# Two-way gated memory of a mixer stage: one triangle over 512 tokens, or two halves with a state across them

## The chip, the cores and the metric

One program runs on one core of one Trainium2 chip. The metric is the device time of a run in microseconds (us). Besides the times there is one profiled run, read here as "the trace". Its times count from the first instruction.

## The reference, cut to what matters

The kernel computes two transformer blocks on 512 tokens of width 1024. The change is in one mixer of the second block, a matrix memory (mLSTM) that runs over the tokens forwards and, a second time, backwards. Eight heads, keys and queries of 64, values of 128:

```python
def step(carry, inp):
    C, n, m = carry
    ...
    s = jnp.einsum('bhtd,bhsd->bhts', qj, kj) * jnp.exp(D - m_t[..., None])
    num = jnp.einsum('bhts,bhsv->bhtv', s, vj) + w_inter[..., None] * jnp.einsum('bhvd,bhtd->bhtv', C, qj)
    den = jnp.sum(s, axis=-1) + w_inter * jnp.einsum('bhd,bhtd->bht', n, qj)
    h = num / jnp.maximum(jnp.abs(den), jnp.exp(-m_t))[..., None]
    ...
    C = decay[..., None, None] * C + jnp.einsum('bhsv,bhsd->bhvd', vj * wk[..., None], kj)
...
h_fwd = mlstm_chunkwise(q, k, v, g[0, 0], jax.nn.log_sigmoid(g[0, 1]))
h_bwd = flip(mlstm_chunkwise(flip(q), flip(k), flip(v), flip(g[1, 0]), flip(jax.nn.log_sigmoid(g[1, 1]))))
hs = (h_fwd + h_bwd).transpose(0, 2, 1, 3).astype(h.dtype)
hs = rms_norm(hs) * head_gain
```

The result does not depend on the chunk: a chunk of 512 needs no state at all, a chunk of 256 needs one state per head and direction.

## The kernel before

Five engines run five queues written out by hand; semaphores order them. **Weights** come in units of 1024 x 256. For unit m, SP loads `raw` (`load(m)`), ScalarE writes its rounded high part (`high(m)`, L839), GpSimd the low part in two halves (`low(m)`, L660), and TensorE multiplies with three matmuls for each tile (L2440 to L2442). Each of raw, high and low has two buffers: `high(m)` waits until TensorE is done with unit m-2. `load(m)` waits for `low(m-2)`. A unit starts on TensorE when its high part and the first half of its low part are there (`unit_ready`).

**The stage od_in** has units n to n+12. n to n+4 give queries, keys (256 features each pair of units) and gates; n+5 to n+8 the output gate `mo`; n+9 to n+12 the values `vx`, each unit for two heads. Gate rows are made by VectorE during n+6 (`gate_rows`): `irow` (log weight of a token as a source), `Mrow` (running maximum), `erow`. After unit n+8 TensorE transposes `irow` (L3234) and then `erow` (L3238), which count `r_tr` to 1 and 2. ScalarE's queue around this is `high(n+8)`, the exponential of `erow` (L1391), two sigmoids of `mo` (L1375), `high(n+9)`, another sigmoid, four silus of `cy` (queries and keys, L1371), `high(n+10)`. SP copies `Mrow` to DRAM (`mrows`) after `load(n+11)` and then reads its 16 rows back, each broadcast to 128 partitions (L642, ring of four).

**The heads.** For head h and direction d (0 forwards, 1 backwards):

- ScalarE (L1431) writes four blocks of weights `wt`, exp(row + column), for the source block j of 128 tokens against all targets at its side: 512, 384, 256, 128 wide forwards, and the reverse backwards. Four sets `wt[s % 4]` exist, s = 2h + d; set s waits for `l_o`, the outputs of s-4.
- GpSimd zeroes half of each diagonal block (L801, 8 a head). Its queue in head h: the 8 selects, `mo` times the gain (L804), in heads 0, 3 and 5 `low(n+11)`, `low(n+12)`, `low(n+13)`, and from head 2 `gated_head(h-2)` (L793).
- TensorE makes scores (L3287), four matmuls 64 rows deep and 512 wide, one in each of banks 0 to 3; `scores_half(h+1, 0)` and `(h+1, 1)` stand in head h. VectorE multiplies weights by scores (`decayed`, L2340, 8 a head), counted by `l_a`.
- TensorE sums (`out_rows(h, d)`, L3273): ten matmuls 128 x 129 over the ten blocks of the triangle. They wait for `l_a` and for `l_h`, VectorE's `heads_out` of the direction before (L2349 to L2359), which empties banks 6 and 7.
- Between these TensorE works off units n+10 to n+12, a third of a block at a time (`next(beside)`): chunks a, b, c of 15, 15 and 18 matmul triples for heads 0 to 5. At the start of a unit it waits for its whole low part (`unit_whole`). Heads 6 and 7 have no such filling.
- VectorE in head h: `decayed` 0 to 4, a copy of values (`take_values`, L2302, heads 1 to 6), `decayed` 5, `heads_out(h-1, 1)`, `decayed` 6 and 7, `heads_out(h, 0)`, and the norm of older heads (`head_sums`, `normed_head`). In head 7 `heads_out(6, 1)` stands after `decayed` 3.
- ScalarE in head h: weights of h, in heads 0, 3, 5 `high(n+11)`, `high(n+12)`, `high(n+13)`, then squares and roots of older heads.

After head 7 come transposes of the normed heads (L3299) and the stage od_out, whose first unit is L2491 and L2496.

Of the kernel before, what the change touches and what calls it, by code (L numbers as in the profile page):

```python
# [220 lines left out]
def bass_block_pair(nc, a, out):  # L221
# [163 lines left out]
    hgain = place("hgain", [P, D], F32, AR + 49408)[0]  # L385
    wt = []
    for i in range(4):
        offset = [ULOFF + 5120 * i] * TB
        for j in range(1, TB):
            offset[j] = offset[j - 1] + 512 * (TB - j + 1 if i % 2 == 0 else j)  # L390
        if i == 3:
            offset = [AR + 57088, ULOFF + 15360, AR + 55552, AR + 53504]
        wt.append([place(f"wt{i}{j}", [P, (TB - j if i % 2 == 0 else j + 1) * P], F32, offset[j])[0] for j in range(TB)])
    cy = place("cy", [P, KC, S], F32, UHOFF)[0]
# [6 lines left out]
    erow = place("erow", [64, S], F32, SQOFF[1])[0]  # L401
    bcr = R + sq
    mrows = nc.dram_tensor("mrows", [64, S], F32, kind="Internal").ap()
    ccol = place("ccol", [P, TB, 64], F32, SSOFF)[0]
    ecol = place("ecol", [P, TB, 64], F32, GSOFF)[0]

# [10 lines left out]
    with ExitStack() as ctx:  # L417
# [13 lines left out]
        def sem(name):  # L431
# [73 lines left out]
        def _(sp):  # L505
# [148 lines left out]
        def _(pool):  # L654
# [164 lines left out]
        def _(act):  # L819
# [580 lines left out]
            nc.scalar.activation(ccol[:], ps[6][:, 0:256].rearrange("p (a b) -> p a b", a=TB), ACT.Copy).then_inc(r_cols, 1)  # L1400
            nc.scalar.activation(ecol[:], ps[7][:, 0:256].rearrange("p (a b) -> p a b", a=TB), ACT.Copy).then_inc(r_cols, 1)
            act.wait_ge(r_cols, 2)

# [17 lines left out]
            nc.scalar.preload_act_table_set("natural_log_exp_and_others")  # L1421
            for h in range(ML_H):
                for d in range(2):
                    s = 2 * h + d
                    act.wait_ge(bc_in[s % BC_RING], 16 * (s // BC_RING + 1))
                    if s >= 4:
                        act.wait_ge(l_o, s - 3)
                    for j in range(TB):
                        lo, hi = (j * P, S) if d == 0 else (0, (j + 1) * P)
                        row = h + 32 * d  # L1430
                        nc.scalar.activation(wt[s % 4][j][:], bcr[s % BC_RING][:, lo:hi], ACT.Exp,  # L1431
                                             bias=ccol[:, j, row:row + 1]).then_inc(l_w, 1)
                if h in (0, 3, 5):
# [23 lines left out]
        def _(dve):  # L1457
# [847 lines left out]
            def gate_rows():  # L2305
# [73 lines left out]
            def mixed_low(j):  # L2379
                low_op(Q0["od_mix"] + j, uL[:, j, :], ps[MIX_BANK[j]][:], uH[:, j, :])  # L2380

            for h in range(ML_H):
                tail = h == ML_H - 1
                for x in range(2 * TB):
                    decayed(8 * h + x)
                    if x == 4 and 1 <= h <= 6:
# [39 lines left out]
        def _(pe):  # L2426
# [795 lines left out]
            for u in range(5, 10):  # L3222
# [8 lines left out]
                if u == 8:  # L3231
# [5 lines left out]
                    for tb in range(TB):  # L3237
                        ins = nc.tensor.transpose(ps[7][:, tb * 64:(tb + 1) * 64], erow[:, tb * P:(tb + 1) * P], ident[0:64, 0:64])  # L3238
                    ins.then_inc(r_tr, 1)
            pe.wait_ge(blk_taken, TAKEN[V_FILL[0]])  # L3240
            pe.wait_ge(r_cols, 2)

# [18 lines left out]
            def out_rows(h, d):  # L3261

                pe.wait_ge(l_a, 8 * h + 4 * d + 4)
                if 2 * h + d:
                    pe.wait_ge(l_h, 2 * h + d)
                if h % 2 == 0 and h and d == 0:
                    pe.wait_ge(blk_taken, TAKEN[V_FILL[0] + h])
                for i in range(TB):
                    dst = ps[6 + i // 2][:, (i % 2) * 129:(i % 2) * 129 + 129]
                    js = range(0, i + 1) if d == 0 else range(i, TB)  # L3270
                    for j in js:
                        at = (i - j if d == 0 else i) * P
                        ins = nc.tensor.matmul(dst, wt[(2 * h + d) % 4][j][:, at:at + P], vx[:, j, h, :],  # L3273
                                               start=(j == js[0]), stop=(j == js[-1]))
                ins.then_inc(l_o, 1)

            pe.wait_ge(c_silu, KC)

            def scores_half(h, d):

                if h >= ML_H:
                    return
                hp = (h % 2) * 64
                for j in range(2 * d, 2 * d + 2):
                    if h:
                        pe.wait_ge(l_a, 8 * (h - 1) + 4 + j + 1)
                    nc.tensor.matmul(ps[j][:], cy[hp:hp + 64, 4 + h // 2, j * P:(j + 1) * P], cy[hp:hp + 64, h // 2, :],  # L3287
                                     start=True, stop=True).then_inc(l_qk, 1)

            def head_transposes(j):  # L3290
# [10 lines left out]

            scores_half(0, 0)
            scores_half(0, 1)
            beside = values_beside()
            for h in range(ML_H):
                next(beside, None)
                scores_half(h + 1, 0)
                next(beside, None)
                if h == ML_H - 1:
                    head_transposes(0)  # L3310
                    head_transposes(1)
                out_rows(h, 0)
                scores_half(h + 1, 1)
                next(beside, None)
# [91 lines left out]
```

## Time and profile before

| | us |
|---|---|
| median of 3 runs | 2059.47 |
| lowest, highest | 2057.3, 2065.16 |
| the profiled execution, first to last instruction | 2057.0 |
| its stretch from the first scores to the first matmul of od_out | 1524.38 to 1645.13 |

The profile gives no separate time of its own run; its span lies 2.5 us below the median. Views used: the page (shares, slices), the chain that ended last in order of time, timelines of one engine (a line that says x20 merges 20 records and its time runs from the first start to the last end), tables of short windows with the granted TensorE clock, and groups of instructions. A matmul in plain fp32 leaves two records, so ten matmuls of `out_rows` are x20.

### The profile page before, as it was taken

The numbers are of one execution on the slowest core, as the hardware profiler recorded it, in microseconds if no ns is written. First come the engines' busy times: TensorE is split into PE (matmuls) and PEld (weight loads), VectorE is DVE, ScalarE is ACT, GpSimd is POOL, SyncE is SP. The second block draws the span as 40 slices with busy tenths as digits, with TensorE's granted clock in tenths as the row PEclk, the third lists the DMA queues.
The fourth block names the chain that finished last, engine by engine and source line by source line (L and its number), as shares of the span: only waits on it lengthen the run. The fifth ranks groups of instructions, "written<-read, shape, count | busy, mean of one in ns | idle before, by whom it ended". The sixth has DMA issues, their size and how long they took to land.

```text
span 2057.0 us, 25915 instructions
## 1 busy us (share of the span) xinstructions
PE 2010.6 (98%) x10087; PEld 1672.1 (81%) x10087; DVE 1199.0 (58%) x1955; ACT 752.2 (37%) x1029; POOL 906.8 (44%) x500
## 2 busy tenths in 40 slices
PE   8999899999999999999999999999999899999998
PEld 6877788988888888877788788888888788888887
DVE  6454657646789895688578877516656752111112
ACT  5344534333513222447542122125353344222121
POOL 3422424754445444346244444445454345444442
PEclk9999999999999999999999999999999999999999
DMA  4322203516577862240348778423341023322321
GB/s 152 102 84 82 77 2 102 165 62 155 146 195 180 200 168 83 82 138 21 87 120 203 187 182 199 128 73 113 103 127 61 21 83 103 103 89 96 103 92 72
DMA packets 227823, 233.41 MB, mean 113 GB/s; under 512 B 6891, under 2 KB 222772, under 8 KB 227580
## 3 DMA queue, kind: packets, MB, share of 16 engines
q1 hardware_dynamic: 227216, 231.72, 40.1%
q8 instruction: 77, 1.26, 0.3%
q14 instruction: 38, 0.31, 0.1%
q10 hardware_dynamic: 492, 0.12, 0.0%
HBM read 229.56 MB, written 2.24 MB: 113 GB/s over the span
## 4 chain that ended last, share of the span: by engine, by line
PE 88%; DVE 7%; issue 2%; ACT 1%; DMA 1%; POOL 1%; SPq 0%; DVEq 0%; ACTq 0%
PE ps L2440 22%; PE ps L2442 21%; PE ps L2441 21%; PE ps L2491 7%; PE ps L2496 3%; DVE adacc L1985 2%; PE ps L3287 1%; PE ps L3273 1%; PE ps L2946 1%; PE ps L2877 1%; POOL wL L660 1%; PE ps L2728 1%; PE ps L2907 1%; DVE ssum L1478 1%; DMA raw<-in_w_in_dram 0%
## 5 line engine op out<-in xcount | busy, mean ns | idle before, releaser
L660 POOL TENSOR_TENSOR wL<-raw,wH 128x1024 fp32r<-128x1024 f32 (+2 forms) x320 | 769.3, 2425 | 948.7 <-ACT wH L839 883.6
L839 ACT ACTIVATE wH<-raw 128x2048 fp32r<-128x2048 f32 (+2 forms) x160 | 300.8, 1880 | 433.3 <-PE ps L2442 331.4
L2440 PE MATMUL ps<-uH,wH 128*128 128x512 f32 x1088 | 425.5, 391 | 3.0 <-DVE uL L1528 0.9
L2442 PE MATMUL ps<-uH,wL 128*128 128x512 f32 x1088 | 423.5, 389 | 0.0
L2441 PE MATMUL ps<-uL,wH 128*128 128x512 f32 x1088 | 423.4, 389 | 0.0
L1985 DVE SCALAR_TENSOR_TENSOR adacc<-adaw,adab,adacc 128x256 f32<-128x256 f32 x372 | 307.6, 827 | 12.9
L2440 PE MATMUL ps<-hnH,wH 128*128 128x512 f32 x728 | 287.7, 395 | 2.2 <-DVE xT L1597 1.7
L2442 PE MATMUL ps<-hnH,wL 128*128 128x512 f32 x728 | 283.8, 390 | 0.0
L2441 PE MATMUL ps<-hnL,wH 128*128 128x512 f32 x728 | 283.2, 389 | 0.0
L2440 PEld LDWEIGHTS ps<-uH,wH 128*128 128x128 f32 x1088 | 204.2, 188 | 46.9 <-issue 3.4
L2442 PEld LDWEIGHTS ps<-uH,wL 128*128 128x128 f32 x1088 | 204.2, 188 | 43.0
L2441 PEld LDWEIGHTS ps<-uL,wH 128*128 128x128 f32 x1088 | 204.3, 188 | 41.9
L2211 DVE TENSOR_TENSOR T<-ps,R 128x512 f32<-128x512 f32 x44 | 30.2, 690 | 280.5 <-PE ps L2442 269.6
L2440 PEld LDWEIGHTS ps<-hnH,wH 128*128 128x128 f32 x728 | 137.0, 188 | 31.4 <-issue 4.1
L2442 PEld LDWEIGHTS ps<-hnH,wL 128*128 128x128 f32 x728 | 136.6, 188 | 28.9
L2441 PEld LDWEIGHTS ps<-hnL,wH 128*128 128x128 f32 x728 | 136.8, 188 | 28.5 <-issue 1.0
L1597 DVE SCALAR_TENSOR_TENSOR xT<-ps,mod,xT 128x512 f32<-128x512 f32 x64 | 47.0, 748 | 148.2 <-PE ps L2442 108.6
L2440 PE MATMUL ps<-wH,hnH 128*128 128x256 f32 x384 | 111.9, 292 | 0.0
L2442 PE MATMUL ps<-wH,hnL 128*128 128x256 f32 x384 | 109.2, 284 | 0.0
L2441 PE MATMUL ps<-wL,hnH 128*128 128x256 f32 x384 | 109.2, 284 | 0.0
L2491 PE MATMUL ps<-hnH,wH 128*128 128x512 f32 x264 | 105.0, 398 | 2.9 <-ACT hnH L888 2.9
L2491 PE MATMUL ps<-hnH,wL 128*128 128x512 f32 x264 | 103.9, 393 | 0.0
(478 smaller groups left out, 3035.3 us busy)
## 6 DMA issues: line engine op xcount, KB each, us to landing
raw<-in_ffn_w_dram SPq DMA_DIRECT2D x60, 1024.0 KB, 5.4
adaw<-in_ada_w_dram SPq DMA_DIRECT2D x192, 256.0 KB, 7.1
raw<-in_w_dram SPq DMA_DIRECT2D x32, 1024.0 KB, 5.5
raw<-in_w_in_dram SPq DMA_DIRECT2D x14, 1024.0 KB, 5.3
raw<-in_od_w_in_dram SPq DMA_DIRECT2D x12, 1024.0 KB, 5.3
raw<-in_w_xkv_dram SPq DMA_DIRECT2D x16, 512.0 KB, 3.6
raw<-in_ffn_w_dram SPq DMA_DIRECT2D x8, 768.0 KB, 4.2
raw<-in_ev_w_in_dram SPq DMA_DIRECT2D x5, 1024.0 KB, 5.3
```

The lines of the kernel that those rows point to most:

```text
L660: nc.gpsimd.tensor_tensor(wL[n % 2][:, k0:k1, 0:c], raw[n % 2][:, k0:k1, 0:c], wH[n % 2][:, k0:k1, 0:c].bitcast(F32), ALU.subtract).then_i ...
L839: nc.scalar.activation(wH[n % 2][:, 0:kc, 0:c], raw[n % 2][:, 0:kc, 0:c], ACT.Copy).then_inc(w_hi, 1)
L1478: nc.vector.tensor_tensor(acc[:], acc[:], sq[q % 2][:], ALU.add).then_inc(sq_added, 1)
L1597: nc.vector.scalar_tensor_tensor(out=xT[:, j, :], in0=ps[b % 4][:], scalar=gate(j), in1=xT[:, j, :], op0=ALU.mult, op1=ALU.add).then_inc(b ...
L1985: ins = nc.vector.scalar_tensor_tensor(out=acc, in0=adaw[m % ADA_RING][:, k, :], scalar=by, in1=acc, op0=ALU.mult, op1=ALU.add)
L2211: nc.vector.tensor_tensor(T[(q0 + c) % 2][:], ps[b % 4][:], R[c][:], ALU.mult).then_inc(blk_taken, 1)
L2440: nc.tensor.matmul(out_ap, wh, xh, start=first, stop=False)
L2441: nc.tensor.matmul(out_ap, wh, xl, start=False, stop=False)
L2442: return nc.tensor.matmul(out_ap, wl, xh, start=False, stop=last)
L2491: nc.tensor.matmul(ps[(BLOCK0[n] + c) % 4][:, 0:tokens], w[n % 2][:, k, cs], xh[:, k, :], start=w is wH and k == 0, stop=False)
L2496: ins = nc.tensor.matmul(ps[(BLOCK0[n] + c) % 4][:, 0:tokens], wH[n % 2][:, k, cs], xl[:, k, :], start=False, stop=k == kc - 1)
L2728: ins = nc.tensor.transpose(ps[6 + g % 2][:, j * P:(j + 1) * P], pr[g % PR_RING][:, j * P:(j + 1) * P], ident)
```

## The change

The tokens are cut into two halves of 256. Inside a half, weights and scores are as before, but only 256 and 128 wide. Across the halves a state of 64 x 129 for each head and direction carries the other half's sum.

```diff
 def scores(h, half):
-    nc.tensor.matmul(ps[j][:], cy[hp:hp + 64, 4 + h // 2, j * P:(j + 1) * P], cy[hp:hp + 64, h // 2, :], ...)
+    nc.tensor.matmul(ps[(2 * h + half) % 3][:, (j % 2) * 2 * P:(j % 2 + 1) * 2 * P],
+                     cy[hp:hp + 64, 4 + h // 2, j * P:(j + 1) * P], cy[hp:hp + 64, h // 2, t0:t0 + 2 * P], ...)
 def out_rows(h, d):
+    for i in (0, 1, 2, 3) if d == 0 else (2, 3, 0, 1):
+        js = range(i // 2 * 2, i + 1) if d == 0 else range(i, i // 2 * 2 + 2)
+        across = i // 2 != d
...
+        if across:
+            if i % 2 == 0:
+                pe.wait_ge(l_kq, ML_H // 2 + h // 2 + 1)
+                pe.wait_ge(h_st, 3 * HG_H + h + 1)
+            ins = nc.tensor.matmul(dst, decayed_queries(h // 2)[hp:hp + 64, i, :], cst_[hp:hp + 64, h // 2 % 2, d, :], ...)
+def states(h):
+    if h % 2 == 0 and h:
+        pe.wait_ge(blk_taken, TAKEN[V_FILL[0] + h])
+    for d in range(2):
+        for j in (2 * d, 2 * d + 1):
+            ins = nc.tensor.matmul(ps[3][hp:hp + 64, ...], weighted_keys(h // 2)[:, j, hp:hp + 64], vx[:, j, h, :], ...)
+    ins.then_inc(h_sp, 1)
```

TensorE's order in head h is now a, `scores(h+1, 0)`, b, `states(h)`, `out_rows(h, 0)`, `scores(h+1, 1)`, c, `out_rows(h, 1)`. Ahead of head 0 it transposes the keys (16 of 128 x 128), and, after unit n+9, `irow` again (4). VectorE weights the keys (4 of 128 x 512, from PSUM) and the queries (4 of 128 x 512); SP stores two decay rows (`erows`) and reads them back in eight broadcasts of 128 KB. ScalarE gets four exponentials on rows, two copies `wcol`, and `states_copy(h)`. Its queue:

```diff
             act.wait_ge(r_rows, 1)
             nc.scalar.activation(erow[:], erow[:], ACT.Exp, scale=-1.0).then_inc(r_em, 1)
+            act.wait_ge(r_rows, 2)
+            nc.scalar.activation(Erow[0:ML_H, 2 * P:S], Mrow[0:ML_H, 2 * P:S], ACT.Exp, bias=rcol[0:ML_H, 0:1]).then_inc(r_em, 1)
...
+            act.wait_ge(r_tr, 1)
+            nc.scalar.activation(irow[0:ML_H, 0:2 * P], irow[0:ML_H, 0:2 * P], ACT.Exp, ...).then_inc(r_em, 1)
...
             output_gate(0)
             output_gate(1)
             high(n+9)
...
+            gate_weights(0)
+            for h in range(ML_H):
+                states_copy(h)
+                if h + 1 < ML_H:
+                    gate_weights(h + 1)
                 if h in (0, 3, 5):
                     high(n + 11 + h // 2)
```

ScalarE, between units n+8 and n+9, before (`wH_51` is written by `high(n+8)`, `wH_52` by `high(n+9)`):

```order
673 L839 ACTIVATE wH_51<-raw_49 128x2048
674 L1391 ACT_TABLE_LOAD
675 L1391 ACTIVATE erow<-erow 64x512
676 L1375 ACT_TABLE_LOAD
677 L1375 ACTIVATE mo<-mo 128x4x256 x2
678 L839 ACTIVATE wH_52<-raw_50 128x2048
```

and now:

```order
673 L867 ACTIVATE wH_51<-raw_49 128x2048
674 L1419 ACT_TABLE_LOAD
675 L1419 ACTIVATE erow<-erow 64x512
676 L1421 ACTIVATE Erow<-Mrow,small 8x256
677 L1422 ACTIVATE Erow<-Mrow,small 8x256
678 L1425 ACTIVATE irow<-irow,Mrow 8x256
679 L1427 ACTIVATE irow<-irow,Mrow 8x256
680 L1403 ACT_TABLE_LOAD
681 L1403 ACTIVATE mo<-mo 128x4x256 x2
682 L867 ACTIVATE wH_52<-raw_50 128x2048
```

Four exponentials stand ahead of the sigmoids and of `high(n+9)`; the first on `irow` (row 678) carries the wait for `r_tr` 1.

ScalarE, end of the weights of head 0 and start of those of head 1, before (`wt_196` to `wt_199` are head 0's backward set, `wt_200` to `wt_203` head 1's forward set, `wH_52` is `high(n+11)`):

```order
694 L1431 ACTIVATE wt_198<-R_71,ccol 128x384
695 L1431 ACTIVATE wt_199<-R_71,ccol 128x512
696 L839 ACTIVATE wH_52<-raw_50 128x2048
697 L1431 ACTIVATE wt_200<-sq_72,ccol 128x512
698 L1431 ACTIVATE wt_201<-sq_72,ccol 128x384
```

and now:

```order
699 L1472 ACTIVATE wt_198<-R_71,ccol 128x128
700 L1472 ACTIVATE wt_199<-R_71,ccol 128x256
701 L1480 ACTIVATE cst__208<-ps 64x258
702 L1472 ACTIVATE wt_200<-sq_72,ccol 128x256
703 L1472 ACTIVATE wt_201<-sq_72,ccol 128x128
704 L1472 ACTIVATE wt_202<-sq_72,ccol 128x256
705 L1472 ACTIVATE wt_203<-sq_72,ccol 128x128
706 L1472 ACTIVATE wt_204<-sq_73,ccol 128x128
707 L1472 ACTIVATE wt_205<-sq_73,ccol 128x256
708 L1472 ACTIVATE wt_206<-sq_73,ccol 128x128
709 L1472 ACTIVATE wt_207<-sq_73,ccol 128x256
710 L867 ACTIVATE wH_52<-raw_50 128x2048
```

`high(n+11)` moved from ahead of head 1's weights to behind them, and all of these behind the copy of head 0's states (row 701). GpSimd's queue has the same order as before. In it `low(n+11)`, which needs `high(n+11)`, stands ahead of head 1's selects:

```order
220 L829 AFFINE_SELECT wt_199<-wt_199 128x128
221 L832 TENSOR_TENSOR mo<-mo,hgain 128x4x128
222 L688 TENSOR_TENSOR wL_54<-raw_50,wH_52 128x1024 x2
223 L829 AFFINE_SELECT wt_200<-wt_200 128x128
224 L829 AFFINE_SELECT wt_201<-wt_201 128x128
```

## Rows read from the trace of the kernel before

**Rows 1.** The page: engine totals; shares of the chain that ended last.
```profile
PE 2010.6 (98%) x10087; PEld 1672.1 (81%) x10087; DVE 1199.0 (58%) x1955; ACT 752.2 (37%) x1029; POOL 906.8 (44%) x500
PE 88%; DVE 7%; issue 2%; ACT 1%; DMA 1%; POOL 1%; SPq 0%; DVEq 0%; ACTq 0%
```
**Rows 2.** The last chain, 1511 to 1648: start us, length us, what.
```profile
1511.20 0.39 PE ps L3234 x4
...
1511.84 0.31 PE ps L2440
...
1523.57 0.77 DVE vx L2302 x2
1524.38 4.67 PE ps L3287 x8
...
1537.08 2.23 PE ps L3273 x20
1539.32 1.91 PE ps L3287 x4
...
1609.18 2.23 PE ps L3273 x20
...
1640.39 0.87 DVE hs L2359 x3
...
1645.13 0.93 PE ps L2491 x4
...
1647.89 0.44 PE ps L3299 x4
```
**Rows 3.** Timeline of ScalarE: start us, length us, what [idle before <-releaser].
```profile
1492.14 1.28 ACT L1375 ACT_TABLE_LOAD   x1
1493.43 2.01 ACT L1375 ACTIVATE mo<-mo 128x1024 f32<-128x1024 f32 x2
1499.78 1.92 ACT L839 ACTIVATE wH<-raw 128x2048 fp32r<-128x2048 f32 x1 [4.33 <-PE ps L2442]
...
1600.35 1.91 ACT L1431 ACTIVATE wt<-R,ccol 128x512 f32<-128x512 f32 x4
```
**Rows 4.** Timeline of GpSimd.
```profile
1530.27 2.01 POOL L801 TENSOR_SCALAR_AFFINE_SELECT wt<-wt 128x128 f32<-128x128 f32 x8
...
1564.14 4.70 POOL L660 TENSOR_TENSOR wL<-raw,wH 128x1024 fp32r<-128x1024 f32 x2 [0.26 <-ACT wH L839]
1568.79 1.27 POOL L793 TENSOR_TENSOR hs<-hs,mo 128x512 f32<-128x512 f32 x1
```
**Rows 5.** Windows: stretch, us, busy of PE, PEld, DVE, ACT, POOL, PEclk, DMA.
```profile
21.00:22.00 1.00, 1.00 (x4) 0.83 (x3) 0.90 (x2) 0.58 (x1) 0.00 (x0) 0.65 0.79 209
...
1526.00:1527.00 1.00, 1.00 (x3) 0.37 (x2) 0.86 (x2) 1.00 (x4) 1.00 (x1) 0.98 0.95 182
...
1533.00:1534.00 1.00, 1.00 (x2) 0.33 (x1) 0.00 (x0) 0.00 (x0) 0.51 (x1) 0.60 1.00 339
...
1630.00:1640.00 10.00, 6.92 (x55) 6.46 (x56) 9.48 (x32) 3.19 (x6) 1.28 (x1) 1.00 0.01 2
```
**Rows 6.** Timeline of TensorE at the program's start.
```profile
17.05 0.77 PE L2491 MATMUL ps<-hnH,wH 128*128 128x512 f32 x1 [2.85 <-ACT hnH L888]
```
**Rows 7.** Timeline of VectorE around `heads_out(5, 1)`.
```profile
1615.60 1.88 DVE L2340 SCALAR_TENSOR_TENSOR wt<-ps,wt 128x512 f32<-128x512 f32 x5
...
1618.38 0.15 DVE L2349 SCALAR_TENSOR_TENSOR small<-ps,ecol 128x2 f32<-128x2 f32 x1
...
1620.53 1.16 DVE L2340 SCALAR_TENSOR_TENSOR wt<-ps,wt 128x384 f32<-128x384 f32 x2
```
**Rows 8.** Groups of instructions by shape, 1510 to 1645: busy us, mean ns.
```profile
L2340 DVE SCALAR_TENSOR_TENSOR wt<-ps,wt 128x512 f32<-128x512 f32 x16 | 10.9, 684 | 1.4 <-PE ps L3287 1.3
...
L2340 DVE SCALAR_TENSOR_TENSOR wt<-ps,wt 128x128 f32<-128x128 f32 x16 | 3.9, 284 | 1.3 <-PE ps L3287 1.3
```
**Rows 9.** DMA issues, 1495 to 1640: KB each, median us to landing.
```profile
R<-mrows SPq DMA_DIRECT2D x8, 256.0 KB, 3.4
```

More of the change, by code:

```diff
@@ L385, in bass_block_pair @@
     hgain = place("hgain", [P, D], F32, AR + 49408)[0]
[L386 to L393, printed above, removed]
+    wt = [[place(f"wt{i}{j}", [P, (2 - j % 2 if i % 2 == 0 else j % 2 + 1) * P], F32,
+                 ULOFF + 3072 * i + 1536 * (j // 2) + (1024 if i % 2 == 0 else 512) * (j % 2))[0] for j in range(TB)] for i in range(4)]
+    cst_ = place("cst_", [P, 2, 2, ML_V + 1], F32, ULOFF + 12288)[0]
     cy = place("cy", [P, KC, S], F32, UHOFF)[0]
@@ L1421, in _, with gate_weights @@
             nc.scalar.preload_act_table_set("natural_log_exp_and_others")
-            for h in range(ML_H):
+            def gate_weights(h):
                 for d in range(2):
@@ L2380, in mixed_low @@
                 low_op(Q0["od_mix"] + j, uL[:, j, :], ps[MIX_BANK[j]][:], uH[:, j, :])
+            dve.wait_ge(r_cols, 4)
+            dve.wait_ge(c_silu, KC)
+            for p in range(ML_H // 2):
+                keys_weighted(p)
+            queries_decayed(0)
             for h in range(ML_H):
@@ L3239, in _ @@
                     ins.then_inc(r_tr, 1)
+            pe.wait_ge(r_em, 5)
+            for tb in range(TB):
+                ins = nc.tensor.transpose(ps[4][:, tb * 64:(tb + 1) * 64], irow[:, tb * P:(tb + 1) * P], ident[0:64, 0:64])
+            ins.then_inc(r_tr, 1)
             pe.wait_ge(blk_taken, TAKEN[V_FILL[0]])
-            pe.wait_ge(r_cols, 2)
+            pe.wait_ge(r_cols, 4)
             def values_beside():
@@ L3275, in out_rows @@
-                ins.then_inc(l_o, 1)
+                for i in (0, 1, 2, 3) if d == 0 else (2, 3, 0, 1):
+                    dst = ps[6 + i // 2][:, (i % 2) * 129:(i % 2) * 129 + 129]
+                    js = range(i // 2 * 2, i + 1) if d == 0 else range(i, i // 2 * 2 + 2)
+                    across = i // 2 != d
+                    for j in js:
+                        at = (i - j if d == 0 else i % 2) * P
+                        ins = nc.tensor.matmul(dst, wt[(2 * h + d) % 4][j][:, at:at + P], vx[:, j, h, :],
+                                               start=(j == js[0]), stop=(j == js[-1] and not across))
+                    if across:
+                        if i % 2 == 0:
+                            pe.wait_ge(l_kq, ML_H // 2 + h // 2 + 1)
+                            pe.wait_ge(h_st, 3 * HG_H + h + 1)
+                        ins = nc.tensor.matmul(dst, decayed_queries(h // 2)[hp:hp + 64, i, :], cst_[hp:hp + 64, h // 2 % 2, d, :],
+                                               start=False, stop=True)
@@ new lines, in out_rows @@
+                ins.then_inc(l_o, 1)
+            def states(h):
+                hp = (h % 2) * 64
+                if h % 2 == 0 and h:
+                    pe.wait_ge(blk_taken, TAKEN[V_FILL[0] + h])
+                if h:
+                    pe.wait_ge(h_st, 3 * HG_H + h)
+                for d in range(2):
+                    for j in (2 * d, 2 * d + 1):
+                        ins = nc.tensor.matmul(ps[3][hp:hp + 64, d * (ML_V + 1):(d + 1) * (ML_V + 1)], weighted_keys(h // 2)[:, j, hp:hp + 64],
+                                               vx[:, j, h, :], start=(j == 2 * d), stop=(j == 2 * d + 1))
+                ins.then_inc(h_sp, 1)
@@ L3277, in _, with scores @@
             pe.wait_ge(c_silu, KC)
-            def scores_half(h, d):
+            def scores(h, half):
                 if h >= ML_H:
@@ L3283, in scores_half, with key_transposes @@
                 hp = (h % 2) * 64
[L3284 to L3287, printed above, removed]
+                if h == 1 and half == 0:
+                    pe.wait_ge(l_kq, 1)
+                if h and half:
+                    pe.wait_ge(l_a, 8 * (h - 1) + 6)
+                elif h >= 2:
+                    pe.wait_ge(l_a, 8 * (h - 1))
+                for j in range(2 * half, 2 * half + 2):
+                    t0 = half * 2 * P
+                    nc.tensor.matmul(ps[(2 * h + half) % 3][:, (j % 2) * 2 * P:(j % 2 + 1) * 2 * P],
+                                     cy[hp:hp + 64, 4 + h // 2, j * P:(j + 1) * P], cy[hp:hp + 64, h // 2, t0:t0 + 2 * P],
                                      start=True, stop=True).then_inc(l_qk, 1)
+            def key_transposes(p):
+                for tb in range(TB):
+                    ins = nc.tensor.transpose(ps[(2, 3, 6, 7)[p]][:, tb * P:(tb + 1) * P], cy[:, 4 + p, tb * P:(tb + 1) * P], ident)
+                ins.then_inc(r_tr, 1)
             def head_transposes(j):
@@ L3300, in head_transposes @@
                 ins.then_inc(n_tr, 1)
-            scores_half(0, 0)
-            scores_half(0, 1)
+            scores(0, 0)
+            scores(0, 1)
+            for p in range(ML_H // 2):
+                key_transposes(p)
             beside = values_beside()
@@ L3306, in _ @@
                 next(beside, None)
-                scores_half(h + 1, 0)
+                scores(h + 1, 0)
                 next(beside, None)
+                if h == 0:
+                    pe.wait_ge(l_kq, ML_H // 2)
+                states(h)
                 if h == ML_H - 1:
```

78 lines of the change are left out of this document (63 added, 15 removed).

## The prediction

> **What bounds the kernel now.** I read the page first: TensorE is busy for 98% of the span and carries 88% of the chain that ended last [rows 1]. So a matmul taken out is worth its time, and any hole put into TensorE's queue costs its length. Then the chain from 1511 to 1648 [rows 2], where all edited work lies. It has four parts. Unit n+9 runs from 1511.84 to 1523.5. The first scores start at 1524.38, after VectorE's copy of values. Heads 0 to 5 repeat every 14.42 us (first `out_rows` of head 0 at 1537.08, of head 5 at 1609.18), and TensorE never waits there. From then on heads 6 and 7 have no filling: VectorE is busy for 9.48 of 10 us and TensorE for 6.92 [rows 5], and the chain alternates between them until `heads_out(7, 1)` ends at 1641.26 and od_out runs from 1645.13 [rows 2].
>
> **TensorE's work in a head.** Two 512-wide scores take 1.91, ten matmuls of 129 columns 2.23, or 0.223 each [rows 2]. A period holds two of each, so the filling is 14.42 - 3.82 - 4.46 = 6.14 (a 1.9, b 1.9, c 2.3). Now each pair of scores is 256 wide: between 0.96 (by columns) and 1.91 (if a fixed part ruled); I take 1.0, since 129-wide matmuls at 0.223 show hardly a fixed part. `out_rows` has six matmuls inside and two across: 8 x 0.223 = 1.8. `states` adds 4 x 0.223 = 0.9. No row has a stationary operand 64 columns wide, but the scores are 64 rows deep; I bound one between 0.11 and 0.3. The period becomes 6.1 + 2.0 + 3.6 + 0.9 = 12.6, 1.8 less, or 9.1 for the five from head 0 to head 5.
>
> **The opening,** from the first scores to the end of `out_rows(0, 0)`: 14.9 before (to 1539.31 [rows 2]). Now scores 2.0, 16 key transposes at 0.11 (four take 0.44 [rows 2]) 1.8, a 1.9, scores 1.0, b 1.9, states 0.9, `out_rows` 1.8: 11.4. That is -3.5, nearly all because the granted clock stood at half from 1527 to 1533.6 before [rows 5] (3.3 lost); that loss may come again (rival 2). Beside it VectorE weights four keys and one pair of queries, each a pass over 512 columns like `decayed` at 0.68 [rows 8] (bounds 0.4 to 0.9), 3.4 in all, under 9 us of TensorE. The four transposes of `irow` (0.39 [rows 2]) and two small copies stand ahead of the first scores, but in parallel with the 0.77 copy of values: +0.1. SP's eight further broadcasts are half the size of those that land in 3.4 [rows 9] and are needed some 5 us after the first scores: nothing.
>
> **The hole ahead of unit n+9.** This is the step that I weigh most. ScalarE's exponential on `irow` waits for `r_tr` 1, since it overwrites what TensorE transposes. That transpose starts at 1511.20 and takes 0.39 [rows 2]. Queued behind the wait are two sigmoids and `high(n+9)`, which before ran at 1499.78 [rows 3], beside unit n+8. Now: wait until 1511.6; two short exponentials 0.8 (nearest: four weight blocks in 1.91 [rows 3], bounds 0.4 to 1.0); table load 1.28; sigmoids 2.01; `high(n+9)` 1.92: 1517.7. GpSimd's first half of `low(n+9)` takes 4.70 / 2 [rows 4]: TensorE may start at 1520.1 in place of 1511.84, **+8.3**. Nothing else is at hand for TensorE. (The table load's row ends at 1493.42 and the sigmoid starts at 1493.43 [rows 3], so a switch costs 1.28 here. The Trainium skill, "ScalarE: Activation LUTs", "What ACT_TABLE_LOAD costs", puts a drain of about 1.38 us on top of each switch; by that the hole would be 9.7 and the sum 1.4 higher. The row has no room for it, so I go by the row.) Later work catches up during the unit: four silus, `high(n+10)`, the last sigmoid and SP's broadcasts (held behind `load(n+11)`, which waits for `low(n+9)`, done at 1522.5) all end before the unit does at some 1534.
>
> **The clock behind it.** At the start of the program TensorE sat idle for 2.85 us, and its matmuls from 17.05 on ran at half the clock (1.2 of 2.4 GHz) until 21.65 [rows 5, 6]: 4.6 us at half, 2.3 lost. An idle stretch of 8.3 will do the same: **+2.3**.
>
> **The holes in heads 1, 4 and 6.** ScalarE now writes the weights of head h+1 only after the copy of head h's states, and in heads 0, 3 and 5 `high` comes behind them. GpSimd's queue is unchanged, so head h+1's selects stand behind the `low` that waits for that `high`. From the end of `states(h)`: copy 0.4, eight weight blocks 3.0 (two sets at 1.5, since 1280 columns in 1.91 [rows 3] shrink to 768; bounds 2.3 and 3.8), `high` 1.9, `low` 4.7, in heads 3 and 5 `gated_head` 1.3, first select 0.3 [rows 4]. Then VectorE: `decayed` 0 to 4, values, `decayed` 5 took 2.78 (1615.60 to 1618.38 [rows 7]) and shed 0.5 (512 columns fewer forwards at 400 ns for 384 [rows 8]), 2.3; I allow 2.5 because the selects feed them at 0.25 each. Then `heads_out(h, 1)` 2.15 [rows 7]. Sum: 15.0 for h = 0, 16.3 for h = 3 and 5. `out_rows(h+1, 0)` waits for this `heads_out`. TensorE has 12.6 of its own work up to there, in head 5 only 12.6 - 3.8 = 8.8. So it stands 2.4 us in head 1 and 3.7 in head 4 (3.0 of these at the start of unit n+12, whose low part is late by the same chain): **+6.1**. In the kernel before ScalarE was a head ahead and none of these waits was late.
>
> **From `out_rows(5, 0)` to `out_rows(6, 0)`** before: 1611.41 to 1620.53, 9.1 (it waited for `heads_out(5, 1)` [rows 2, 7]). Now 16.3 - 1.8 = 14.5: **+5.3**, with TensorE idle for most of 7 us. From there to the end of `heads_out(7, 1)` the chain is VectorE's: head 7's weights are 1024 columns narrower (-1.0), one `out_rows` on the chain is shorter (-0.4): -1.5. Behind it nothing changes.
>
> **The clock in the tail.** It stayed at 1.00 there with TensorE 69% busy [rows 5]. Now a hole of 5 to 6 us comes first, as long as or longer than the one of rows 6. At half the clock `out_rows(6, 0)` costs 1.8 more; if the clock stays low to the end of the stage, each of four `out_rows` does, less their slack beside VectorE: 4.2. I take **+2.0**.
>
> **Sum against the profiled execution** (span 2057.0): 8.3 + 2.3 + 0.1 - 3.5 - 9.1 + 6.1 + 5.3 - 1.5 + 2.0 = +10.0: 2067.0. The median lies 2.5 above the span: 2069.5, with the upward bounds weighing more, **2070 us**, 0.5% more than before. About 0.5%, 10.3 us, is what a measurement of this kernel can tell from no change, so the forecast lies on that edge. Chance 0.45 for 2066 to 2073.
>
> **Rival 1, the saving comes through (faster).** TensorE sheds 3.5 + 9.1 + 1.5 with 0.1 added: -14, 2045.5. It decides for itself if ScalarE gets over the wait on `r_tr` without TensorE noticing, that is if `high(n+9)` need not wait, and if `low` is done before the selects are missed. For it: 98% busy TensorE [rows 1]. Against: both waits are plain in the queues, and the hole would need to be under a tenth of what I find. Chance 0.05. If only the holes in the heads fail to show (weights and `high` early enough), 8.3 + 2.3 + 0.1 - 3.5 - 9.1 - 1.5 = -3.4: 2056. Chance 0.10.
>
> **Rival 2, the clock falls more often.** The first scores again follow a gap and are light work; the clock may fall as at 1527 [rows 5], +3.3, and stay low through the tail, +2.2 more: 2075.5. For it: the same sequence did so before; against: the scores are half as long and followed by full-height transposes. Chance 0.22.
>
> **Rival 3, small matmuls don't pay.** If a half-wide score pair kept 1.91 in place of 1.0, the opening would cost 2.7 more and the five periods 9.1, less 3.6 that the holes in heads 1 and 4 would swallow: +8.2, 2078. Chance 0.04.
>
> **Rival 4, the clock holds in the tail and idle work is shorter than I think:** 2062 to 2066. Chance 0.14.
>
> **Chances.** Slower by over 0.5% (above 2069.8): over half of the likeliest case, rivals 2 and 3: 0.55. Within 0.5%: 0.38. Faster by over 0.5%: 0.07. The range 2060 to 2079 leaves out rival 1 alone.
>
> **What would show it.** In the trace after: TensorE idle for some 8 us between the `erow` transposes and the next unit, released by GpSimd's low part; the clock at half right behind it; ScalarE idle until the `irow` transposes; the distance between first `out_rows` of heads at 12.6 for heads 1 to 2 and 2 to 3, some 15 and 16 where it crosses into heads 1 and 4; a hole of about 6 us ahead of head 6, with `high` and `low` between weights and selects. The forecast is wrong if unit n+9 starts within 2 us of `erow`'s transposes, or if the selects of heads 1, 4 and 6 follow their weights at once.

## The result and the profile after

| | median, us | lowest to highest | profiled span |
|---|---|---|---|
| before (4 runs) | 2058.6 | 2057.3 to 2065.16 | 2057.0 |
| after (4 runs) | 2077.07 | 2076.08 to 2078.29 | 2074.4 |

The ratio is 1.0091 (95% interval 1.0072 to 1.0109): the change costs 0.9%, or 17.4 us between the two profiled spans (18.5 between the medians). The forecast was 2070 with a range of 2060 to 2079, so the sign and the range held, and the size was too small by 7 us.

The page of the kernel after, engine totals and shares of the last chain, against [rows 1]:

```profile
PE 2014.8 (97%) x10107; PEld 1682.6 (81%) x10107; DVE 1200.3 (58%) x1964; ACT 747.2 (36%) x1043; POOL 905.5 (44%) x500
PE 88%; DVE 6%; ACT 2%; issue 2%; POOL 1%; DMA 1%; SPq 0%; DVEq 0%; ACTq 0%
```

Fewer columns are multiplied, and yet TensorE's busy time rose from 2010.6 to 2014.8. These totals can't tell why: the answer lies in single stretches.

**The hole ahead of unit n+9.** Timeline of ScalarE after (start us, length us, what, [idle before <-releaser]), to be read against [rows 3]:

```profile
1492.47 0.51 ACT L1422 ACTIVATE Erow<-Mrow,small 8x256 f32<-8x256 f32 x1
1511.56 0.51 ACT L1425 ACTIVATE irow<-irow,Mrow 8x256 f32<-8x256 f32 x1 [18.58 <-PE ps L3312]
...
1512.62 1.28 ACT L1403 ACT_TABLE_LOAD   x1
1513.91 2.00 ACT L1403 ACTIVATE mo<-mo 128x1024 f32<-128x1024 f32 x2
1515.82 1.89 ACT L867 ACTIVATE wH<-raw 128x2048 fp32r<-128x2048 f32 x1
```

The same stretch on GpSimd:

```profile
1517.79 4.68 POOL L688 TENSOR_TENSOR wL<-raw,wH 128x1024 fp32r<-128x1024 f32 x2 [22.66 <-ACT wH L867]
```

And on TensorE:

```profile
1511.36 0.41 PE L3316 MATMUL ps<-cst,erow 64*128 64x64 f32 x4
1520.23 0.55 PE L2518 MATMUL ps<-wH,hnH 128*128 128x256 f32 x1 [8.46 <-issue]
```

One wait, released by `irow`'s transposes (L3312), held ScalarE for 18.58 us. `high(n+9)` (L867) came at 1515.82 in place of 1499.78, GpSimd's low part 22.66 us after its last work, and unit n+9 began at 1520.23 in place of 1511.84. The profile labels TensorE's idle time "issue". That it is a wait for the low half is seen from GpSimd's row: half of 4.68 us after 1517.79 is 1520.13.

**The clock.** Windows (stretch, us, busy of PE, PEld, DVE, ACT, POOL, then PEclk, DMA share and GB/s), against [rows 5]:

```profile
1516.00:1517.00 1.00, 0.00 (x0) 0.00 (x0) 0.00 (x0) 1.00 (x1) 0.00 (x0) 0.61 0.00 0
1520.00:1523.00 3.00, 2.77 (x13) 2.80 (x14) 0.00 (x0) 3.00 (x5) 2.47 (x2) 0.50 0.02 5
...
1534.00:1546.00 12.00, 11.93 (x82) 10.24 (x82) 6.21 (x15) 6.23 (x16) 3.55 (x9) 1.00 0.90 227
...
1628.00:1634.00 6.00, 2.39 (x10) 2.01 (x11) 5.72 (x22) 0.77 (x3) 3.78 (x10) 0.57 0.54 176
1634.00:1648.00 14.00, 12.99 (x49) 10.20 (x49) 7.82 (x32) 4.03 (x13) 4.46 (x10) 0.50 0.00 0
```

The granted clock fell to half (1.2 of 2.4 GHz) inside the hole at 1516, and only some 3 us of work ran at half behind it. In the opening (1534 to 1546) it stayed at 1.00, where the kernel before had half from 1527 to 1533.6. From about 1629 to 1649 it stood at half again; before, it was 1.00 there.

**The heads.** The last chain after (start us, length us, what), against [rows 2]. L3374 is `states`, L3355 a 128-row matmul of `out_rows`, L3361 one across the halves (64 rows), L3393 a score:

```profile
1534.07 1.99 PE ps L3393 x8
...
1543.82 1.09 PE ps L3355 x8
1544.91 0.42 PE ps L3361 x2
1545.32 0.64 PE ps L3355 x4
1545.96 0.30 PE ps L3361
1546.27 0.76 PE ps L3393 x4
...
1571.43 1.02 PE ps L3374 x8
...
1585.41 1.04 PE ps L3374 x8
...
1602.99 1.13 PE ps L3355 x8
...
1615.99 1.04 PE ps L3374 x8
...
1617.94 2.46 ACT wt L1472 x7
1620.39 1.80 ACT wH L867
...
1633.59 2.06 PE ps L3355 x8
```

The undisturbed period is 1585.41 - 1571.43 = 13.98, against 14.42 before. `out_rows(0, 0)` takes 1546.27 - 1543.82 = 2.45, with eight matmuls of 129 columns; before, ten of them took 2.23. The pieces show where: two records of L3361 are one matmul and take 0.42, four of L3355 are two and take 0.64. At 0.223 each they would be 0.22 and 0.45. So each change between 64 and 128 rows adds 0.2. The first eight records show the same price for a change of width: they follow `states`, whose stationary operand is 64 columns wide, and take 1.09, where eight of the ten records that follow a filling in `out_rows(0, 1)` take 0.89 (1.12 for the ten). The chain passes to ScalarE (weights, then `high`) ahead of heads 4 and 6, as forecast. From there it reaches VectorE's next work over the norm of an older head and not over `low`, which ran beside it and ended its part about 0.6 us sooner (last section). TensorE's timeline shows the holes in heads 1, 4 and 6:

```profile
1558.44 1.13 PE L3355 MATMUL ps<-vx,wt 128*128 128x129 f32 x8 [0.63 <-DVE hs L2430]
...
1596.55 0.36 PE L2518 MATMUL ps<-wH,hnH 128*128 128x256 f32 x1 [2.18 <-POOL wL L688]
...
1631.15 1.98 PE L3374 MATMUL ps<-vx,kw 128*64 128x129 f32 x8 [5.34 <-DVE vx L2357]
```

**Where the 17.4 us are**, by the milestones of the two traces: to the first scores +9.7 (1534.07 against 1524.38); opening to the end of `out_rows(0, 0)` -2.7 (12.2 against 14.9); five periods +1.1 (1546.27 to 1619.5 is 73.2, against 72.1), which is 5 x -0.44 and holes of 3.3; from `out_rows(5, 0)` to `out_rows(6, 0)` +5.0 (14.1 against 9.1); from there to the end of `heads_out(7, 1)` +4.4 (25.1 against 20.7). That is 17.5.

### The profile page after: what moved, and what is told of

The parts are those of the page before. It is cut to its first block, busy times and chain, and to the rows that moved or that the text cites. A ratio compares the mean times of both kernels' runs of the same rounds, so it can differ in the third digit from the quotient of the medians.

```text
span 2074.4 us, 26013 instructions
## 1 busy us (share of the span) xinstructions
PE 2014.8 (97%) x10107; PEld 1682.6 (81%) x10107; DVE 1200.3 (58%) x1964; ACT 747.2 (36%) x1043; POOL 905.5 (44%) x500
## 4 chain that ended last, share of the span: by engine, by line
PE 88%; DVE 6%; ACT 2%; issue 2%; POOL 1%; DMA 1%; SPq 0%; DVEq 0%; ACTq 0%
PE ps L2518 22%; PE ps L2520 21%; PE ps L2519 21%; PE ps L2569 7%; PE ps L2574 4%; DVE adacc L2040 1%; PE ps L3024 1%; PE ps L3355 1%; PE ps L2955 1%; POOL wL L688 1%; PE ps L2806 1%; PE ps L2985 1%; ACT wH L867 1%; DVE ssum L1533 1%; PE ps L3361 1%
## 5 line engine op out<-in xcount | busy, mean ns | idle before, releaser
L867 ACT ACTIVATE wH<-raw 128x2048 fp32r<-128x2048 f32 (+2 forms) x160 | 300.6, 1878 | 429.6 <-PE ps L2520 326.7
L2518 PE MATMUL ps<-uH,wH 128*128 128x512 f32 x1088 | 426.0, 392 | 3.1 <-DVE uL L1583 0.9
L2518 PE MATMUL ps<-hnH,wH 128*128 128x512 f32 x728 | 288.1, 396 | 1.7 <-DVE xT L1652 1.7
L2518 PEld LDWEIGHTS ps<-uH,wH 128*128 128x128 f32 x1088 | 204.4, 188 | 47.1 <-issue 3.5
L2518 PEld LDWEIGHTS ps<-hnH,wH 128*128 128x128 f32 x728 | 137.1, 188 | 30.6 <-issue 3.5
L2518 PE MATMUL ps<-wH,hnH 128*128 128x256 f32 x384 | 112.1, 292 | 10.6 <-issue 8.5
```

Of the source, the lines that this page charges most:

```text
L867: nc.scalar.activation(wH[n % 2][:, 0:kc, 0:c], raw[n % 2][:, 0:kc, 0:c], ACT.Copy).then_inc(w_hi, 1)
L2518: nc.tensor.matmul(out_ap, wh, xh, start=first, stop=False)
```

## Experiments

All kernels are edits of the kernel after. The first four shared a chip with 14 runs of the kernel before (median 2056.84), the next three with 8 (2057.95), the last with 9 (2059.3). The kernel after was timed in a session of its own (before 2058.6 there), so a difference between medians of two sessions carries some 2 us; the ratios to the kernel before are the safer comparison. Theory: the order of ScalarE's queue makes the holes, changes between 64 and 128 rows eat the savings, and the clock falls where TensorE's work is thin. Rivals: the broadcasts or VectorE set these holes (e1 and e2 leave both as they are, and the holes go); the small matmuls cost a fixed time whatever stands beside them (e5 and e6); and the hole itself, not the clock, is what the tail pays (e4).

### e1_irow_late: the wait on the transposes behind the last sigmoid

```diff
-            act.wait_ge(r_tr, 1)
-            nc.scalar.activation(irow[0:ML_H, 0:2 * P], irow[0:ML_H, 0:2 * P], ACT.Exp, ...)
-            nc.scalar.activation(irow[32:32 + ML_H, 2 * P:S], irow[32:32 + ML_H, 2 * P:S], ACT.Exp, ...)
             output_gate(0)
...
             output_gate(3)
+            act.wait_ge(r_tr, 1)
+            nc.scalar.activation(irow[0:ML_H, 0:2 * P], ...)
+            nc.scalar.activation(irow[32:32 + ML_H, 2 * P:S], ...)
             act.wait_ge(r_tr, 2)
```

> The changed kernel with ScalarE's two exponentials on irow, and their wait for TensorE's transposes, moved from ahead of high(n+9) to behind the last sigmoid. Theory (the wait holds high(n+9), and with it unit n+9): the 8.4 us hole between 1511.6 and 1520.2 goes, and the half clock behind it (some 1.5 us): about 10 us less than the changed kernel, 2067. The rest of the stage keeps its lengths; if the clock falls in the opening, as in the kernel before, 2070. Rival (the unit waits for something else, SP's loads or GpSimd): the hole stays and the time is within 2 us of 2077.

Measured: 2068.23 (2065.95 to 2069.24, 4 runs), ratio to before 1.0047 (1.003 to 1.0063), 8.8 under the kernel after. ScalarE's and TensorE's timelines:

```profile
1499.86 1.92 ACT L867 ACTIVATE wH<-raw 128x2048 fp32r<-128x2048 f32 x1 [3.40 <-PE ps L2520]
```

```profile
1511.51 0.41 PE L3316 MATMUL ps<-cst,erow 64*128 64x64 f32 x4
1511.85 0.38 PE L2518 MATMUL ps<-wH,hnH 128*128 128x256 f32 x1
```

`high(n+9)` is back at 1499.86 and unit n+9 follows the transposes without a gap; the first scores start at 1524.47, 9.6 sooner. So the hole and the half clock behind it are that one wait, shown. The profiled span fell by only 6.9, since the clock then fell at a place where it had not fallen after:

```profile
1588.00:1594.00 6.00, 6.00 (x24) 4.94 (x23) 5.76 (x22) 0.00 (x0) 3.59 (x9) 0.50 0.90 257
```

That is some 3 us lost behind the 2.2 us hole of head 4.

### e2_high_first: `high` ahead of the copy of states and the weights

```diff
             for h in range(ML_H):
+                if h in (0, 3, 5):
+                    high(n + 11 + h // 2)
                 states_copy(h)
                 if h + 1 < ML_H:
                     gate_weights(h + 1)
-                if h in (0, 3, 5):
-                    high(n + 11 + h // 2)
```

> The changed kernel with high(n+11), high(n+12), high(n+13) ahead of the states' copy and of the next head's weights in heads 0, 3 and 5. Theory (high and low stand between the states and the next head's selects): TensorE's holes ahead of out_rows of heads 1, 4 and 6 shrink from 0.7, 2.6 and about 6 us to under 1 each except head 6 (2 to 3, VectorE), and the clock stays at full in the tail, worth some 6: 2064. Rival (VectorE's own work sets the distance): under 3 us change.

Measured: 2066.15 (2063.07 to 2070.25, 5 runs), ratio 1.0045 (1.0028 to 1.0063), 10.9 under the kernel after; span 2064.4, 10.0 less. `states` of heads 0 to 5 start every 13.98 to 13.99 us with no hole, and the one ahead of head 6 shrank:

```profile
1624.21 1.09 PE L3374 MATMUL ps<-vx,kw 128*64 128x129 f32 x8 [0.22 <-DVE vx L2357]
1626.66 1.13 PE L3355 MATMUL ps<-vx,wt 128*128 128x129 f32 x8 [1.35 <-DVE hs L2430]
```

From the first scores to `out_rows(6, 0)` it takes 91.1 in place of 99.5, -8.4; that is all of the holes (3.3 + 5.0). The tail takes 22.2 in place of 25.1, with the clock at half for 7 us instead of 20:

```profile
1626.00:1632.00 6.00, 3.70 (x24) 2.93 (x25) 3.63 (x14) 3.46 (x11) 2.85 (x8) 1.00 0.00 1
1632.00:1639.00 7.00, 7.00 (x31) 5.76 (x30) 6.65 (x23) 1.33 (x4) 1.89 (x4) 0.52 0.00 0
```

### e3_both: both edits

> Both edits together. Theory: they add, 10 and 13 us: 2054, and 2057 if the clock falls in the opening; so between the same as and 0.3% faster than the kernel before. Rival (matmuls among 64-row ones cost so much that nothing of the smaller triangle is left): 2059 or more.

Measured: 2056.39 (2053.64 to 2060.21, 10 runs), ratio 0.9994 (0.9984 to 1.0004): no difference from before. The two gains add: 0.44 and 0.46 points of the ratio against 0.97, or 9.1 and 9.5 us against 20, with intervals of some 3.5 us to either side of each. So moving work within one engine's queue takes back the whole net loss. What is left is a change without holes that still saves nothing, so the saved columns must be lost elsewhere. The tail is one such place, though no long hole precedes it:

```profile
1614.00:1631.00 17.00, 15.65 (x59) 12.89 (x60) 9.77 (x37) 6.08 (x17) 5.71 (x11) 0.51 0.00 0
```

### e4_fill_hole: unused matmuls in the hole ahead of head 6

```diff
+                if h == 6:
+                    pe.wait_ge(blk_taken, TAKEN[V_FILL[0] + 5])
+                    for x in range(13):
+                        parts(ps[bank(V_FILL[0] + 4)][:, 0:UC], ...)
                 states(h)
```

> The changed kernel with 39 matmuls 256 wide (4.7 us) whose result nobody reads, put into TensorE's hole ahead of the states of head 6; all waits stay. Theory (the tail is long because the clock stands at half from 1629 to 1649 behind that hole): the clock stays at 1.00, the tail from out_rows(6, 0) to the first matmul of od_out falls from about 29 to 23 to 24 us, total 2071.5. Rival (the tail is long by its added matmuls and waits): no change, or up to 1 us more.

Measured: 2073.15 (2072.58 to 2075.0, 4 runs), ratio 1.0073 (1.0056 to 1.009). In its profiled run all work ahead of the edit lay 1.5 us later than in the kernel after (unit n+9 starts at 1521.77), so lengths are counted from the first scores (1535.90). From there to the first od_out matmul in TensorE's timeline it takes 119.9, against 122.8 (to 1656.86): -2.9, all of it behind `out_rows(6, 0)`, which starts equally late (99.6 against 99.5 from the first scores). The clock stayed at 1.00 until 1641.5 and then fell for 6.5 us; the window in it:

```profile
1642.00:1648.00 6.00, 6.00 (x24) 4.99 (x24) 5.55 (x21) 1.68 (x5) 1.11 (x2) 0.50 0.00 0
```

So the hole's length is set by the chain over ScalarE and VectorE and not by TensorE, and 2.9 us of the tail are the clock that fell in it. (The same milestone in the kernel before is 1639.29, or 114.9 from the first scores; 1645.13 in its table and in [rows 2] is the first od_out matmul on the last chain, behind which three groups of od_out had already run.) The expected 5.5 was too much: the clock still fell for 6.5 us, later.

### e5_across_full and e6_all_full: no 64-row matmuls

```diff
-                        ins = nc.tensor.matmul(dst, decayed_queries(h // 2)[hp:hp + 64, i, :], cst_[hp:hp + 64, h // 2 % 2, d, :],
+                        ins = nc.tensor.matmul(dst, decayed_queries(h // 2)[:, i, :], vx[:, 0, h, :],
```

e6 has this and the scores over all 128 rows:

```diff
-                                     cy[hp:hp + 64, 4 + h // 2, j * P:(j + 1) * P], cy[hp:hp + 64, h // 2, t0:t0 + 2 * P],
+                                     cy[:, 4 + h // 2, j * P:(j + 1) * P], cy[:, h // 2, t0:t0 + 2 * P],
```

> The changed kernel with the matmuls across the halves 128 rows deep in place of 64 (their operands are other data of the same width, so the states drop out of the result); count, order and waits stay. Theory (going between 64-row and 128-row matmuls costs about 0.2 us each way): out_rows falls from 2.4 to about 1.8 us and the period from head 2 to head 3 from 14.0 to 12.9. Rival (a small matmul has a fixed price, or the waits cost): out_rows stays above 2.2.

> As the run before, with the scores 128 rows deep too (two heads' products summed, so the scores are not the reference's). Theory: no 64-row matmul is left beside the fillings, the four half scores and the fillings behind them lose another 0.6 us a head, the period is about 12.3. Rival: the period stays as in the run before, since 256 columns cost what they cost.

Measured, in one run each: 2074.06 (span 2072.3) and 2069.5 (span 2067.8). Both compute something else than the reference and serve only to measure lengths. The length in question is the distance between `states` of heads 2 and 3, whose starts are 1572.28 and 1585.32 in e5, and 1570.57 and 1582.82 in e6: **13.04** and **12.25**, against 13.98. Columns and instructions are the same in all three, only the rows differ. A head has ten changes between 64 and 128 rows in the kernel after: two around `scores(h+1, 0)`, three in `out_rows(h, 0)`, which ends on 64 rows as the scores behind it begin, one ahead of c, four in and behind `out_rows(h, 1)`. In e5 it has four, in e6 none: 0.94 / 6 = 0.16 and 0.79 / 4 = 0.20 us each (e7 shows why the first is lower). The rival, a fixed cost of small matmuls, would leave the period at 13.98. The totals fell less than five periods' worth, since the holes of heads 1, 4 and 6 grew (0.6, 2.2, 5.3 to 2.4, 3.3, 6.5 in e6): the chain over ScalarE and GpSimd keeps its length.

### e7_both_grouped: e3, and each half's across matmuls side by side

```diff
-                for i in (0, 1, 2, 3) if d == 0 else (2, 3, 0, 1):
-                    js = ...
-                    across = i // 2 != d
+                for half in (0, 1) if d == 0 else (1, 0):
+                    across = half != d
+                    for i in (2 * half, 2 * half + 1):
+                        for j in js:
+                            ins = nc.tensor.matmul(dst[i % 2], wt[(2 * h + d) % 4][j][:, at:at + P], vx[:, j, h, :], ...)
+                    if across:
+                        for i in (2 * half, 2 * half + 1):
+                            ins = nc.tensor.matmul(dst[i % 2], decayed_queries(h // 2)[hp:hp + 64, i, :], ...)
```

> Both moves of ScalarE's work, and in out_rows the two matmuls across the halves one behind the other, after all 128-row ones of their bank. Theory (each change of row depth costs): one 64-row run in place of two in each out_rows, 0.3 to 0.4 us less each, 5 us or less over 16 of them where TensorE is the limit (heads 0 to 5, 12 of them: 4): 2050 if e3_both gives 2054. Rival: no change against e3_both.

Measured: 2050.25 (2048.04 to 2051.39, 5 runs), ratio 0.9955 (0.9939 to 0.9972). It beats the kernel before by 0.45%, and the interval leaves out 1. Its last chain (L3375 `states`, L3356 and L3362 the two kinds of `out_rows`):

```profile
1560.41 1.02 PE ps L3375 x8
...
1573.41 1.02 PE ps L3375 x8
1574.44 1.54 PE ps L3356 x12
...
1579.40 1.34 PE ps L3356 x12
1580.74 0.64 PE ps L3362 x4
```

The period is 13.00, with four changes fewer than in e3, which is 0.98 less. The same matmuls in another order take 1 us less per head. Not all of it is changes, as TensorE's timeline shows (L3394 is a score, L2518 the filling behind it):

```profile
1575.90 0.37 PE L3362 MATMUL ps<-cst__208,hs 64*128 64x129 f32 x1
1575.92 0.48 PE L3394 MATMUL ps<-cy 64*128 64x256 f32 x1
1576.12 0.38 PE L3362 MATMUL ps<-cst__208,hs 64*128 64x129 f32 x2
1576.24 0.38 PE L3394 MATMUL ps<-cy 64*128 64x256 f32 x1
...
1576.97 0.39 PE L2518 MATMUL ps<-wH,hnH 128*128 128x256 f32 x1
```

The two matmuls across the halves use one half of the 128 rows, and the scores of the next head, which follow them, the other. Their records start 0.02 us apart, and the two kinds together take 1.07, which is one change (0.2) and the 0.86 that a pair of scores takes alone in e6. So both matmuls across run beside the scores for nothing; in the kernel after and in e3 only the last one does (1574.53 for L3361, 1574.53 for L3393). That is 0.22 us a head which e7 gains on top and e5, whose matmuls across use all rows, loses. With it a change costs (0.98 - 0.22) / 4 = 0.19 in e7 and (0.94 + 0.22) / 6 = 0.19 in e5, as the 0.20 of e6.

### e8_grouped_busy: e7 with unused matmuls in the two gaps of head 6

```diff
+                if h == 6:
+                    unused(4)
                 out_rows(h, 0)
...
+                if h == 6:
+                    unused(5)
                 out_rows(h, 1)
```

`unused(n)` runs 3n matmuls like e4's.

> e7 again, with 12 unused matmuls of 256 columns (0.12 each at full clock, 1.4 us) put between states(6) and out_rows(6, 0), where TensorE stood idle for 1.35 us in e7, and 15 more (1.8 us) ahead of out_rows(6, 1), where it stood idle for 1.87; their sums are read by nobody. In e7 TensorE ran at half its clock from 1611.6 to 1614.7 and from 1618.5 to 1625, though no long hole came before. Theory A, thin work alone brings the clock down in this stage: with the two gaps filled the clock stays at 1.00 until head_transposes or further, and the first od_out matmul comes 2 to 4 us sooner than e7's 1631.90; about 2047. Theory B, the work in the gaps does not decide it (the 64-row or 64-column matmuls themselves draw the low clock): the half-clock stretch stays as long, the unused matmuls run at half (0.21 each) and cost 1 to 2 us; 2051 to 2052.

Measured: 2049.31 (2048.36 to 2054.34, 5 runs), ratio 0.9949 (0.9936 to 0.9963), which overlaps e7's. Windows of e7:

```profile
1611.00:1615.00 4.00, 3.36 (x17) 3.17 (x19) 1.12 (x4) 3.44 (x11) 0.88 (x1) 0.57 0.01 2
...
1618.00:1625.00 7.00, 7.00 (x33) 6.21 (x32) 5.95 (x23) 1.75 (x5) 1.29 (x2) 0.51 0.00 0
```

And of e8:

```profile
1625.00:1630.00 5.00, 3.24 (x24) 2.79 (x24) 4.79 (x17) 3.60 (x6) 1.27 (x1) 1.00 0.00 0
...
1631.00:1634.00 3.00, 3.00 (x13) 2.55 (x13) 1.98 (x4) 0.00 (x0) 0.00 (x0) 0.50 0.00 0
```

Half of theory A came true. The clock stayed at 1.00 from 1600 until 1630, and from `states(5)` to `states(7)` it took 19.0 in place of 21.8. But then it fell, to half from 1630.3 to about 1637, under `out_rows(7, 1)` and od_out, which are TensorE's alone, and by the first od_out matmul the gain was gone (32.5 against 32.6 from `states(5)`). The low stretch moved, and no time was won.

## Why the prediction was right, and where it failed

**The hole ahead of n+9, +8.3: right**, term by term. Measured 8.4 (1520.23 against 1511.84): exponentials 1.06 (0.8 taken), table load 1.28, `high` 1.89. The sigmoid at 1513.91 starts 0.01 after the load's end, so the row of before was the right guide, and the 1.38 us drain that the Trainium skill puts on top ("ScalarE: Activation LUTs", "What ACT_TABLE_LOAD costs") isn't seen here either. e1 shows the cause.

**The clock behind it, +2.3: too much**, 1.3 (9.7 to the first scores less 8.4). The clock recovered after 3 us of work; behind the same hole it took 3.4 in e4 and 6.2 in e2, so the size was within what this code does from run to run.

**The opening, -3.5: nearly**, -2.7. The half-clock stretch of before didn't come back. The miss is `out_rows(0, 0)`: 2.45 where 1.8 was taken.

**The period, 12.6 us: the step that failed.** It was 13.98. The words were "8 x 0.223 = 1.8" and "I bound one between 0.11 and 0.3". I priced the matmuls one by one by their columns, and took the price from ten alike in a row. What costs is the change of height between neighbours, about 0.2 us each. The kernel before has four of them in a head, around its two pairs of scores, and the rows that I used had these in them; the change adds six. e5, which has the four alone, shows the share of the six: 13.04, so they are 0.94 of the 1.38 missed. The other 0.44 is small matmuls priced too low: in e5 the fillings took 6.15 (6.14 forecast), scores 2.1 (2.0), `out_rows` 3.8 (3.6, with 0.2 for the change of width behind `states`) and `states` 1.0 (0.9). The prediction looked for it in the wrong place: rival 3 put it on the scores, which in fact took 0.76 and 1.06. The Trainium skill has the rule ("TensorEngine Tiling (Array Packing)", "Key Properties"): "Changing tiling mode (not just tile) drains the TensorE". I hadn't weighed it; the traces of e5, e6 and e7 agree in that each change costs about 0.2 us, but whether that is a drain they don't show. Five periods lost 6.9 us of the forecast 9.1.

**The holes in heads 1 and 4, +6.1: right chain, smaller hole.** From the end of `states` to the next `out_rows`, head 1 took 14.6 (15.0 forecast) and head 4 16.5 (16.3). The holes came to 3.3, since TensorE was busy for longer meanwhile. The two misses partly cancel: -9.1 + 6.1 = -3.0 was forecast, +1.1 measured. e2 shows the cause, the place of `high` in the queue.

**`out_rows(5, 0)` to `out_rows(6, 0)`, +5.3: right**, +5.0, with the idle time of 5.34 ahead of `states(6)`, released by VectorE.

**The tail, -1.5 and +2.0: mis-sized.** +0.5 was forecast, +4.4 measured. The clock stood at half for 20 us. The row [rows 5] had it at 1.00 with TensorE 69% busy, and I took half of the 4.2 bound. With 13 us less of it the tail took 2.9 less (22.2 in e2, 22.1 in e4), so at least 2.9 of the 4.4 are the clock's. The other 1.5 may be the 7 us at half that were left there; if VectorE's -1.5 came through as well, the clock cost 5.9 in all, above my bound of 4.2. No run separates these two. The cause of the fall is only half settled. e4 and e8 show that work put into the gaps delays it. But e3 runs `out_rows(6, 0)` at half behind a gap of 1.35 us where e2 runs it at full behind the same gap, and what decides between these two stays open.

**Rivals.** The saving came through only in e7 (2050), without holes and with fewer changes of height. Rival 3 (2078) came nearest in total and had the right kind of cause, small matmuls that don't pay, in the wrong place. Of rival 2 (2075.5) one half came true: the clock stayed low in the tail, but did not fall in the opening.

**Luck.** The likeliest stretch, 2066 to 2073, was missed. That 2077 lies inside the stated range owes something to errors of opposite sign: the periods (+6.9) and the tail (+3.9) cost more than forecast, the holes in heads 1 and 4 (-2.8) and the clock behind n+9 (-1.0) less. The sign did not need luck: the holes alone (+8.4, +3.3 and +5.0) outweigh what the opening and the periods gained (-2.7 and -2.2), and e1 and e2 show what makes them.

## What to carry to other kernels

A wait put into an in-order queue is paid by what stands behind it. Ask of each new wait which weights, two engines on, come after it: here moving two waits and what they hold in ScalarE's queue was worth 20 us and left the arithmetic alone. Price a small matmul with its neighbours: 64-row and 128-row matmuls that alternate pay about 0.2 us per change, so group them, and where two groups use opposite halves of the rows put them next to each other, since they then overlap (e7). And filling a gap to keep the clock up is worth time only if the low stretch doesn't then land where TensorE is the bound.

## What the runs showed of the hardware

VectorE's operations on 128 x 4 elements, 0.16 to 0.22 us elsewhere, stretched while GpSimd's `low` ran beside them. VectorE after, in head 5:

```profile
1623.42 1.23 DVE L2443 TENSOR_SCALAR adab<-small 128x4 f32<-128x4 f32 x1
1624.68 2.26 DVE L1563 TENSOR_TENSOR adab<-small 128x4 f32<-128x4 f32 x1
1626.97 1.18 DVE L1564 SCALAR_TENSOR_TENSOR adab<-adab 128x4 f32<-128x4 f32 x1
```

GpSimd at the same time:

```profile
1622.27 4.65 POOL L688 TENSOR_TENSOR wL<-raw,wH 128x1024 fp32r<-128x1024 f32 x2 [10.85 <-ACT wH L867]
```

In e2, where `low` isn't beside them, the same three took 0.19, 0.21 and 0.22. Before, one of them took 1.22 beside GpSimd's multiplication:

```profile
1642.08 1.22 DVE L1508 TENSOR_TENSOR adab<-small 128x4 f32<-128x4 f32 x1
```

Each ended with a piece of GpSimd's: at 1624.65, 1626.94 and 1628.15, where the two halves of `low` ended at about 1624.6 and 1626.92, and `gated_head` behind it at 1628.14. No run took this apart. Here it mattered little: GpSimd's first select starts at 1628.09, in head 1 VectorE went on 0.38 us after the start of such a select, and here it did at 1629.10, when the norm was done. So the stretched norm made the hole about 0.6 us longer than the `low` alone would have.
